# A two-block transformer kernel on one core: a weight split moved, attention's value products and reciprocals regrouped, experts with 17 chunk slots

## The reference

```python
h = _modulate(_rms(x, norm1_g[l]), sh1, sc1)
hc = _modulate(_rms(ctx, norm1_g[l]), csh1, csc1)
p = h @ w_in[l]
pc = hc @ w_in[l]
...
pr = jax.nn.softmax(s, axis=-1)
return jnp.einsum('bhqk,bkhd->bqhd', pr, v)
...
gate, idx = lax.top_k(jnp.swapaxes(aff, 1, 2), cap)
xe = jax.vmap(lambda hb, ib: hb[ib])(h, idx)
a = jnp.einsum('becd,edf->becf', xe, w_g)
u = jnp.einsum('becd,edf->becf', xe, w_u)
ye = jnp.einsum('becf,efd->becd', jax.nn.silu(a) * u, w_d) * gate[..., None]
return jax.vmap(lambda yb, ib: jnp.zeros((T, D)).at[ib.reshape(-1)].add(yb.reshape(-1, D)))(ye, idx)
```

## Time and profile before

| what | value |
|---|---|
| runs | 1329.82, 1331.42, 1329.75 us; median 1329.82 |
| profiled execution, own time | 1330.76 us |
| its span | 1328.9 us (1328.95 in the list of cores) |
| mean granted clock of PE | 0.993 |
| busy share: PE, DVE, ACT, POOL | 98%, 51%, 35%, 33% |
| w_lo of a chunk on POOL (L892) | 79 times, mean 4.626 us |
| w_hi of a chunk on ACT (L1742) | 80 times, mean 1.908 us |
| expert products (L1469, into gate, up) | 488 times, mean 0.596 us |
| the two reductions of gate columns (L2665, L2666) | start at 585.90 and 586.07, 0.15 and 0.16 us |
| rate of the DMAs during the experts | 420 GB/s |

### The profile page before, as it was taken

How to read it: one execution, slowest core, us unless ns; L and a number is a source line. 1 busy time by engine, 2 the same in 40 slices (tenths; PEclk the granted TensorE clock), 3 DMA queues, 4 the chain that set the end, 5 groups by cost and what they waited for, 6 DMA issues and landing times.

```text
span 1328.9 us, 15718 instructions
## 1 busy us (share of the span) xinstructions
PE 1305.9 (98%) x6306; PEld 960.4 (72%) x6306; DVE 682.6 (51%) x1254; ACT 468.1 (35%) x633; POOL 433.7 (33%) x136
## 2 busy tenths in 40 slices
PE   8989999999999899999999999999999999999998
PEld 5779888865588844444447788888888888888887
DVE  2456987757783633343346656612461551551553
ACT  4345223345621221121135671433242331431443
POOL 3144244247612000000015334444245345344340
PEclk9989999999999899999999999999999999999999
DMA  9521199201025799999993113222132222223201
GB/s 371 219 95 64 56 356 345 99 1 64 32 95 190 283 366 421 420 421 421 420 394 127 64 64 127 96 95 95 64 127 95 95 96 95 95 95 105 85 1 64
DMA packets 33764, 226.55 MB, mean 170 GB/s; under 512 B 3872, under 2 KB 4512, under 8 KB 7712
## 3 DMA queue, kind: packets, MB, share of 16 engines
q1 hardware_dynamic: 32256, 218.79, 42.6%
q0 software_dynamic: 1152, 4.19, 0.9%
q10 hardware_dynamic: 288, 2.62, 0.5%
HBM read 221.40 MB, written 4.19 MB: 170 GB/s over the span
## 4 chain that ended last, share of the span: by engine, by line
PE 89%; DVE 6%; ACT 2%; DMA 1%; POOL 1%; issue 1%; SPq 0%; DVEq 0%; ACTq 0%
PE psum L958 22%; PE psum L960 21%; PE psum L959 21%; PE psum L1469 13%; PE psum L1277 1%; PE psum L1243 1%; PE psum L1454 1%; PE psum L1457 1%; POOL w_lo L892 1%; DMA x<-in_x 1%; PE psum L1005 1%; PE psum L1541 1%; PE psum L1429 1%; ACT w_hi L1742 1%; DVE rs L2463 1%
## 5 line engine op out<-in xcount | busy, mean ns | idle before, releaser
L892 POOL TENSOR_TENSOR w_lo<-raw,w_hi 128x2048 fp32r<-128x2048 f32 x79 | 365.4, 4626 | 588.2 <-ACT w_hi L1742 588.1
L958 PE MATMUL psum<-b_hi,w_hi 128*128 128x512 f32 x608 | 238.2, 392 | 0.1
L960 PE MATMUL psum<-b_hi,w_lo 128*128 128x512 f32 x608 | 236.8, 389 | 0.0
L959 PE MATMUL psum<-b_lo,w_hi 128*128 128x512 f32 x608 | 236.7, 389 | 0.0
L1742 ACT ACTIVATE w_hi<-raw 128x2048 fp32r<-128x2048 f32 x80 | 152.6, 1908 | 150.4 <-PE psum L960 108.1
L958 PEld LDWEIGHTS psum<-b_hi,w_hi 128*128 128x128 f32 x608 | 114.1, 188 | 30.7 <-issue 5.7
L960 PEld LDWEIGHTS psum<-b_hi,w_lo 128*128 128x128 f32 x608 | 114.1, 188 | 24.0
L959 PEld LDWEIGHTS psum<-b_lo,w_hi 128*128 128x128 f32 x608 | 114.2, 188 | 23.1
L1469 PE MATMUL psum<-ex_ring,xe 128*64 128x512 f32 x488 | 108.8, 596 | 0.9 <-ACT xe L1973 0.9
L2511 DVE TENSOR_TENSOR x<-psum,x 128x512 f32<-128x512 f32 x39 | 26.9, 691 | 127.9 <-PE psum L960 127.9
L958 PE MATMUL psum<-h_hi,w_hi 128*128 128x512 f32 x200 | 82.6, 413 | 5.0 <-POOL w_lo L892 3.7
(11 more groups left out here) (440 smaller groups left out, 2288.9 us busy)
## 6 DMA issues: line engine op xcount, KB each, us to landing
raw<-in_stream SPq DMA_DIRECT2D x97, 1024.0 KB, 4.9
ex_ring<-in_stream SPq DMA_DIRECT2D x89, 1024.0 KB, 18.3
mod_in<-in_stream SPq DMA_DIRECT2D x8, 1024.0 KB, 20.8
ex_last<-in_stream SPq DMA_DIRECT2D x7, 1024.0 KB, 17.7
x<-in_x SPq DMA_DIRECT2D x4, 512.0 KB, 6.7
x<-in_x ACTq DMA_DIRECT2D x1, 2048.0 KB, 8.6
xt<-h2t SPq DMA_DIRECT2D x8, 256.0 KB, 10.4
out<-y_out SPq DMA_DIRECT2D x4, 512.0 KB, 3.0
```

What stands on the lines that cost most here:

```text
L892: nc.gpsimd.tensor_tensor(w_lo[:, slot, :], raw[:, raw_slot, :], w_hi[:, slot, :].bitcast(F32), ALU.subtract).then_inc(w_lo_done, 1)
L958: mm(o, w[0], x[0], start=start, stop=False)
L959: mm(o, w[0], x[1], start=False, stop=False)
L960: return mm(o, w[1], x[0], start=False, stop=stop)
```

## The change

It has three parts.

1. **Context.** In ACT's loop over the context's high parts, `split_weights` is called after the fourth, so chunk 3 is split there and no longer behind the squares of the query tiles.
2. **Attention.** All three value pairs of a head stand in one burst at its end. ACT takes the output of head h-1 behind the exponential of k = 1 instead of k = 2. The reciprocal and its multiplication are cut into two token halves: DVE does the first in the even head and the second in the odd head that follows. The last pair's halves come one after the other.
3. **Experts.** The ring has 17 slots; two more chunks (16 in place of 14) are issued ahead of the xt writes, the seventeenth behind them. Pairs 0 and 1 keep gate values of their own. For pairs 2 to 7 the ids' products have six columns instead of two, with the gate columns among them, and DVE reduces them there; it frees four matmuls per pair. The one-hot and its comparison stand ahead of the gate products for pairs 1 to 7. Five combine tiles stand behind the ids and none behind the gate products. The gathered tokens have two buffers instead of four, the scaled expert outputs (`ye_hi`, `ye_lo`) one instead of two; a table `tok_affs` holds ids and affinities together; two tiles are padded to 128 partitions and set to zero.

```diff
@@ -42,7 +42,7 @@
-NEX = 15
+NEX = 17
...
@@ -190,8 +190,8 @@
-EX_SLOT = EX_W[5:] + [10, 11, 12, 13, 14] + EX_RAW + EX_W[:5]
-EX_FIRST = [6, 7, 8, 9, 10, 11, 12, 13, 14, 0, 1, 2, 3, 4, 5]
+EX_SLOT = EX_W[2:] + [10, 11, 12, 13, 15, 16, 14] + EX_RAW + EX_W[:2]
+EX_FIRST = [11, 12, 13, 14, 15, 16, 0, 1, 2, 3, 4, 5, 6, 7, 8, 9, 10]
...
@@ -276,7 +276,9 @@
-BEHIND_YE, BEHIND_GATE, BEHIND_UP, BEHIND_ACT = (0, 1, 2), (3, 4), (5, 6), (7,)
+BEHIND_YE, BEHIND_UP, BEHIND_ACT = (0, 1, 2, 3, 4), (5, 6), (7,)
+OWN_GATES = 2
+GATE_COLUMNS = (2, 0, 3, 1, *range(4, PAIRS))
...
@@ -394,12 +396,19 @@
+    def places(i):
+        if i < OWN_GATES:
+            p.add("gates", i, by=("gcol_done", GATE_COLUMNS.index(i) + 1), bank=5)
+        p.add("onehot", i, bank=6)
...
-        combine(i - 1, BEHIND_YE, (5, 6, 7))
+        combine(i - 1, BEHIND_YE, (5, 6, 7, 1, 2))
+        if i >= 1:
+            places(i)
...
-        p.add("gates", i, bank=5)
-        p.add("onehot", i, bank=6)
-        combine(i - 1, BEHIND_GATE, (7, 5))
+        if i == 0:
+            places(i)
...
@@ -582,7 +591,8 @@
-        rs = at("rs", R + 98, [P, T])
+        rs_first = at("rs_first", R + 98, [P, FH])
+        rs_second = [at("rs_second0", R + 99, [P, FH]), at("rs_second1", R + 31, [P, FH])]
...
@@ -600,22 +610,21 @@
-        xg = at("xg", R + 32, [P, 4, D])
-        tokid = at("tokid", R + 126.5 + 184 / 256, [P, TT, 2], F32R)
+        xg = at("xg", R + 32, [P, 2, D])
...
-        ex_last = at("ex_last", R + 64, [P, CH])
-        ye_hi = at("ye_hi", R + 72, [P, 2, D], F32R)
-        ye_lo = at("ye_lo", R + 80, [P, 2, D], F32R)
+        ex_more = [at(f"ex_more{i}", R + kb, [P, CH]) for i, kb in enumerate((64, 40, 80))]
+        ye_hi = at("ye_hi", R + 72, [P, D], F32R)
+        ye_lo = at("ye_lo", R + 76, [P, D], F32R)
...
-        slots_r = at("slots_r", R + 120, [NE, T], F32R)
...
+        slots_r = at("slots_r", R + 120, [P, T], F32R)
...
@@ -897,11 +909,11 @@
-                    if i >= 4:
-                        pool.wait_ge(tile_full, TILE["xe", i - 4, 1] + 1)
+                    if i >= 2:
+                        pool.wait_ge(tile_full, TILE["xe", i - 2, 1] + 1)
...
-                        out=xg[:, i % 4, :], out_offset=None, in_=xt_d,
-                        in_offset=bass.IndirectOffsetOnAxis(ap=ids[:, i:i + 1], axis=0)).then_inc(gathered[i % 4], 16)
+                        out=xg[:, i % 2, :], out_offset=None, in_=xt_d,
+                        in_offset=bass.IndirectOffsetOnAxis(ap=ids[:, i:i + 1], axis=0)).then_inc(gathered[i % 2], 16)
...
@@ -1300,22 +1312,19 @@
                     done(mm3(o, (k_hi[b][:, tok], k_lo[b][:, tok]), (q_hi[b][:], q_lo[b][:]), True, True))
-                    if k == 2 and h >= 1:
-                        pv_pair(h - 1, KT - 2)
-                        if h % 2 == 0:
-                            prob_sums(h // 2 - 1)
+                    if k == 2 and h >= 2 and h % 2 == 0:
+                        prob_sums(h // 2 - 1)
                     if k >= 2 and h + 1 < H:
                         max_pair(h + 1, k - 2)
-                pv_pair(h, 0)
-                pv_pair(h, 2)
+                for k in range(0, KT, 2):
+                    pv_pair(h, k)
                 if h + 1 < H:
...
                     head_t(h + 2)
-            pv_pair(H - 1, KT - 2)
             prob_sums(H // 2 - 1)
             att_x = lambda k: (att_hi[:, k, :], att_lo[:, k, :])
...
@@ -1416,17 +1425,20 @@
+                n = 2 if i < OWN_GATES else 6
+                if n == 6:
+                    pe.wait_ge(affs_done, 1)
...
-                    last = mm(o[:, 0:2], pick_tok[:, i % 4, t, :], tokid[:, t, :], start=t == 0, stop=t == TT - 1)
+                    last = mm(o[:, 0:n], pick_tok[:, i % 4, t, :], tok_affs[:, t, i, 0:n], start=t == 0, stop=t == TT - 1)
...
-                pe.wait_ge(gathered[i % 4], 16 * (i // 4 + 1))
+                pe.wait_ge(gathered[i % 2], 16 * (i // 2 + 1))
...
-                    last = nc.tensor.transpose(o[:, k * P:(k + 1) * P], xg[:, i % 4, (4 * u + k) * P:(4 * u + k + 1) * P],
+                    last = nc.tensor.transpose(o[:, k * P:(k + 1) * P], xg[:, i % 2, (4 * u + k) * P:(4 * u + k + 1) * P],
...
@@ -1435,8 +1447,7 @@
-                    last = mm(o[:, 0:4], pick_tok[:, i % 4, t, :], affs[:, t, 4 * i:4 * i + 4],
-                              start=t == 0, stop=t == TT - 1)
+                    last = mm(o[:, 0:4], pick_tok[:, i % 4, t, :], tok_affs[:, t, i, 2:6], start=t == 0, stop=t == TT - 1)
...
@@ -1499,9 +1518,8 @@
-                gate_values(i)
-                onehot(i)
-                combined(BEHIND_GATE)
+                if i == 0:
+                    places(i)
...
@@ -1801,6 +1819,8 @@
                 hi_of_pre(hc_hi[:, j, :], pre[:, j % 2, 0:TC], bias=mod[:, j, 1:2])
+                if j == 3:
+                    split_weights(TILE["ckv", KL - 1] + 1)
             act.wait_ge(consts_in, 16 * 4)
...
@@ -1885,8 +1905,11 @@
-                    act.wait_ge(att_done, j)
-                A(rs[:], o, ACT.Copy).then_inc(freed_act, 1)
+                    act.wait_ge(att_half, j)
+                A(rs_first[:], o[:, 0:FH], ACT.Copy)
+                if j >= 2:
+                    act.wait_ge(att_done, j - 1)
+                A(rs_second[j % 2][:], o[:, FH:T], ACT.Copy).then_inc(freed_act, 1)
...
@@ -1906,10 +1929,10 @@
-                    if k == 2 and h >= 1:
+                    if k == 1 and h >= 1:
...
-                        if h % 2 == 0:
-                            output_sums(h // 2 - 1)
+                    if k == 2 and h >= 2 and h % 2 == 0:
+                        output_sums(h // 2 - 1)
...
@@ -1988,11 +2011,11 @@
-                act.wait_ge(freed_dve, PLAN.freed_count(TILE["gates", i]))
+                act.wait_ge(gcol_done, GATE_COLUMNS.index(i) + 1)
...
-                    hi(ye_hi[:, i % 2, half * T:half * T + T], bank("ye", i, half), scale=gcol[:, i:i + 1])
+                    hi(ye_hi[:, half * T:half * T + T], bank("ye", i, half), scale=gcol[:, i:i + 1])
...
@@ -2456,12 +2479,14 @@
-            def pair_output(j):
-                dve.wait_ge(freed_act, PLAN.freed_count(TILE["sums", j]))
-                dve.wait_ge(o_sum, 2 * j + 2)
-                link(V.reciprocal(rs[:], rs[:]))
-                V.tensor_tensor(att[:, j, :], att[:, j, :], rs[:], ALU.mult).then_inc(att_done, 1)
+            def pair_output(j, s):
+                if s == 0:
+                    dve.wait_ge(freed_act, PLAN.freed_count(TILE["sums", j]))
+                    dve.wait_ge(o_sum, 2 * j + 2)
+                r, tok = (rs_first, rs_second[j % 2])[s], slice(s * FH, s * FH + FH)
+                link(V.reciprocal(r[:], r[:]))
+                V.tensor_tensor(att[:, j, tok], att[:, j, tok], r[:], ALU.mult).then_inc((att_half, att_done)[s], 1)
...
@@ -2480,12 +2505,13 @@
-                if h >= 2 and h % 2 == 0:
-                    pair_output(h // 2 - 1)
+                if h >= 2:
+                    pair_output(h // 2 - 1, h % 2)
...
-            pair_output(H // 2 - 1)
+            for s in range(2):
+                pair_output(H // 2 - 1, s)
...
@@ -2569,7 +2595,10 @@
-            V.tensor_copy(tokid[:].rearrange("p t c -> p (t c)"), col("tok", 0, 2 * TT))
+            V.tensor_copy(tok_affs[:, :, :, 0:2], col("tok", 0, 2 * TT).rearrange("p (t c) -> p t c", c=2).unsqueeze(2)
+                          .to_broadcast([P, TT, PAIRS, 2]))
+            V.memset(slots_r[:].bitcast(F32), 0.0)
+            V.memset(pair_r[:].bitcast(F32), 0.0)
...
@@ -2608,7 +2637,7 @@
-                    full(dve, "gates", i - 4)
+                    full(dve, "gates" if i - 4 < OWN_GATES else "ids", i - 4)
...
@@ -2618,7 +2647,19 @@
-                V.tensor_copy(ids[:, i:i + 1], take("ids", i)[:, 0:1]).then_inc(ids_done, 1)
+                o = take("ids", i)
+                if i >= OWN_GATES:
+                    gate_columns(i, o[:, 2:6])
+                V.tensor_copy(ids[:, i:i + 1], o[:, 0:1]).then_inc(ids_done, 1)
+            def gate_columns(i, o):
+                V.tensor_reduce(gcol[0:CAP, i:i + 1], o[0:CAP, 0:2], AX.X, ALU.add)
+                V.tensor_reduce(gcol[CAP:P, i:i + 1], o[CAP:P, 2:4], AX.X, ALU.add).then_inc(gcol_done, 1)
+            def places(i):
+                if i < OWN_GATES:
+                    gate_columns(i, take("gates", i))
+                free(V.tensor_scalar(place[:, i % 2, :], take("onehot", i), col("slot"), None, ALU.is_equal))
...
@@ -2627,15 +2668,20 @@
+            ins = V.tensor_tensor(slots_r[0:NE, :], slots[:], chosen[:], ALU.mult)
...
+            aff_2 = aff[:].rearrange("p t (i e) -> p t i e", e=2)
+            for t in range(TT):
+                ins = V.tensor_copy(tok_affs[:, t, :, 2:6:2], aff_2[:, t, :, :])
+            link(ins)
+            for t in range(TT):
+                ins = V.tensor_tensor(tok_affs[:, t, :, 3:6:2], aff_2[:, t, :, :], tok_affs[:, t, :, 2:6:2].bitcast(F32),
+                                      ALU.subtract)
```

(10 more changed lines are left out.)

36 lines of the change are left out of this document (19 added, 17 removed).

## The result

The changed kernel takes 1332.91 us (median of 20 runs, 1329.73 to 1337.71), the kernel before 1329.59 (20 runs, 1326.85 to 1331.52). The ratio is 1.0026, with a 95% interval of 1.0018 to 1.0035. The profiled execution of the changed kernel took 1337.71 us, the longest of its 20; it shows the losses at their largest, and 4.8 us of it are not in the median. The ratios and their intervals are not quotients of the two medians printed beside them and differ from those by up to 0.07%.

The account below looks back on a forecast made before the run. PE, busy 98% of the span, was taken as the bound. Terms -1.4 +1.8 -3.6 +2.7 +0.8 = +0.3 gave 1331.1 us for the profiled execution, 1330.1 for the median; range 1319.5 to 1336.

Parts of the forecast that it names:

- rival C: Experts' start and context: late xt delays the gather by 4, clock falls in both; +4.8 on the forecast, 1334.9; chance 0.16.
- Context, -1.4: Context: stall of 3.4 removed, 3.4 made by held hc_lo; clock saving 0 or -2.7, middle taken: -1.4 us.
- Attention, +1.8: Attention: k_lo waits gone -1.3, multiplications held by POOL in heads 3 and 5 +3.0, last head +0.1: +1.8 us.
- Experts on PE, -3.6: Expert pairs: one group of small products between pairs instead of two, with a one-hot wait of 0.45: -3.6 us together.
- The start, +2.7 and +0.8: Experts' start: two chunks ahead of xt delay the first gather, transposes 2.7 us later; possible clock fall +0.8.
- A: Whole change works: DVE not held, xt's delay hidden; -11.0 us, 1318.8; chance 0.17.
- B: Moves only swap stalls, but the clock stays up in the context and before the experts: 1328.0; chance 0.25.
- D: Experts: ring does not get ahead, weight stream sets their end, the 3.6 us are lost: 1333.7; chance 0.05.

Follow-up runs that it names:

- experts_15_slots: The kernel before with the experts' part alone, keeping the ring of 15 slots and its slot lists: 1330.55 us, ratio 1.001.
- attention_only: The kernel before with only the attention's part of the change (value products in one burst, halved reciprocals): 1331.19 us, ratio 1.0021.
- experts_only: The kernel before with only the experts' part of the change: 1331.68 us, ratio 1.0015.
- both_halves_even: The kernel before with the attention's part alone, both halves of reciprocal and multiplication done in the even head: 1331.31 us, ratio 1.0017.
- extra_behind_xt: The kernel before with the experts' part alone, its two extra chunks issued behind the xt writes: 1325.62 us, ratio 0.9974.
- extra_behind_gather: The kernel before with the experts' part alone, its two extra chunks issued only after the first gather has landed: 1327.49 us, ratio 0.999.
- idle_44: The kernel before with the experts' part alone, 44 idle products instead of 16 ahead of the first transposes: 1331.36 us, ratio 1.0014.
- pool_behind_product: The kernel before with the attention's part alone, POOL's low part behind heads 3 and 5 waiting for DVE's second multiplication: 1328.94 us, ratio 0.9998.
- changed_extra_behind_xt: The changed kernel with only the two extra chunks moved behind the xt writes: 1327.23 us, ratio 0.999 against the kernel before.
- context_only: The kernel before with only the context's split moved behind the fourth high part: 1328.75 us, ratio 0.9992.
- split_after_eight: The kernel before with chunk 3 split behind the context's eighth high part: 1326.92 us, ratio 0.9983.

## Why the prediction was right or wrong

The forecast was 1330.1, no change; the kernel is at 1332.9, in the range and between the forecast and rival C (1334.9). The change is slower by a little more than what I had called measurable, so the likeliest case named the wrong side of that line. By its steps:

- **Context, -1.4.** The mechanism was right: hc_lo over 4 us beside the low part, the eighth part 3.4 late as forecast; four pieces of stop forecast, three found, 2.4 us of stops, and slower products for the rest. The rule of the Trainium skill that was weighed there (SBUF — State Buffer, "Who interferes with whom") agrees with these rows: 4.52 us beside 4.58. I had asked whether the clock falls or not; it fell for a shorter time. But the 2.7 that I took as the clock's loss before was that of one profile: behind the same stop, profiles of other kernels with the same early part lost about 1 us less six times and nothing once. The part alone measured -0.6. The raw chunk at 173 us, which I had not looked at, may take some back; that is read from two stops of 0.38 and 0.50, not tested.
- **Attention, +1.8.** The part alone measured +1.9 by the medians (+2.8 by the ratio, 1.1 to 4.5), but the terms are not mine, and the agreement is luck. One meeting and not two: head 3's multiplication escaped by 0.04 to 0.06 us, as the burst brings DVE there sooner than I had it: its addition begins 3.15 us ahead of head 4 (317.01 against 320.16) and not 2.37 (318.94 against 321.31). The one that met cost 2.1 and not 1.5, in some executions with the clock on top, which I had put at nothing here. I had the last head at 0.1; it waits 0.84 for POOL.
- **Experts on PE, -3.6.** Measured -4.0. The one-hot waits 0.19 (four times) or 0.40 (twice), not 0.45; the span from the ids to the gate is 3.62, as forecast (3.63). That the slots are needed held: 3.7 us of waits without them. The buffers and memsets that I had put at nothing made no new stop in the pairs.
- **The start, +2.7 and +0.8.** This is the step that failed. xt landed as forecast (14.9 us, I had said 15), but I left the gather at 4.4 from issue to landing where it took 5.9: later by 4, it meets the picks of the next pairs on DVE, and its instruction takes 2.6. The transposes came 4.1 later and not 2.7. I had looked for what a low part of POOL's holds on DVE, and not for what DVE holds on POOL. (That the picks do it is read from three timelines; no run moved them.) And I gave the clock's fall less than half a chance behind a stop of 2.7; with stops of 4.14 and 4.44 it fell in both profiles that have them and cost 2.6. These are the terms of rival C (4 and 2.9). With them in the sum (+3.2) the forecast would have been 1333.3.
- **Rivals.** A is out: no stop vanished without another. B is out for the experts. D is out for this order, where the extra chunks are issued ahead of the gather; with 15 slots it holds, and with 17 filled only behind the gather it does by 1.1 us. C is nearest to what happened, at the start of the experts; its longer fall in the context did not come, and the stop of 2.1 us in head 6 and its clock are in none of the rivals.

## What to carry to other kernels

Where a load only has to be early and a write is waited for, put the write first on their queue: the same two chunks made this kernel 5 us slower, and the experts' part alone 5 to 6, ahead of the write than behind it. In these traces a DVE instruction with two SBUF inputs that begins behind a low part of GpSimd's ends with it or within 0.6 us behind it (0.43 us became 4.55), so order the two by a wait rather than by luck. A stop that lowers the clock in some executions only shows up as a wide spread of the times, and a profile is one draw of it: look at several before putting a price on the clock. When an engine saves time in a stage that is fed by a stream, give the stream as much lead as the saving, and look at what the lead displaces.

## What the runs showed of the hardware

- The stop of 3.38 us ahead of the earlier trace rows's restart was followed by a granted clock of 0.74 over 77 to 90 us in the profile of before, and of experts_15_slots. It was 0.87 in those of attention_only, experts_only, both_halves_even, extra_behind_xt, extra_behind_gather and idle_44, and 1.00 in that of pool_behind_product, all with the same early part and a stop of 3.38 or 3.39. From the first context product to the Fourier branch these took 43.3 and 43.5, 42.2 to 42.3, and 40.6 us. So the same stop costs up to 2.8 us more or less from one execution to another. After a stop of 2.14 us in head 6 the clock fell to 0.59 over 350 to 360 us in the changed kernel; after 2.15 and 2.12 us in attention_only and changed_extra_behind_xt it stayed at 1.00. A stop of 1.82 us in context_only was followed by 0.60 over 70 to 73 us, one of 1.95 in split_after_eight by 1.00 over 77 to 90. A stop's price in clock is a chance, not a sum.
- The hold goes both ways. The gather's instruction on POOL took 1.12 us in before, behind the picks, and 2.60, 2.00 and 2.23 (idle_44) where it began inside them, ending 0.97 or 0.98 after their end each time. Head 3's low part, begun 0.04 us behind a multiplication of 0.43, took 4.84 where 4.58 is usual.
- The first gather landed in 4.4 us where no chunk was under way (before, extra_behind_gather), in 6.0 beside two chunks of 1 MB (extra_behind_xt), and the later gathers of before, beside the full stream, in 8.5 to 9.9.
